# Projections and experts' gate/up in products of 512 columns instead of 256

## The reference

```
def swiglu(h, w_gate, w_up, w_down):
    return (jax.nn.silu(h @ w_gate) * (h @ w_up)) @ w_down
```

## Time and profile before

| | |
|---|---|
| median of 3 runs | 2544.52 us (2544.34 to 2544.85) |
| the profiled execution's own time | 2551.51 us |
| its span, first to last instruction | 2549.70 us, mean granted TensorE clock 0.966 |
| TensorE matmul busy | 2403.7 us (94%) |
| VectorE busy | 1775.0 us (70%) |
| ScalarE busy | 1316.0 us (52%) |
| GpSimd busy | 190.2 us (7%) |
| read from memory | 539.03 MB, 212 GB/s over the span |

### The profile page before, as it was taken

One profiled execution on the slowest core, in us unless ns is written; L12 is line 12 of the kernel. 1 busy time (PEld: TensorE's weight loads), 2 busy tenths in 40 slices (PEclk: granted clock), 3 DMA queues, 4 the chain that ended last, 5 costly groups with the idle time before them and its releaser, 6 DMA issues. The chain is left out here.

```text
span 2549.7 us, 45461 instructions
## 1 busy us (share of the span) xinstructions
PE 2403.7 (94%) x17555; PEld 2189.1 (86%) x17555; DVE 1775.0 (70%) x2869; ACT 1316.0 (52%) x2067; POOL 190.2 (7%) x168
## 2 busy tenths in 40 slices
PE   7889999999998999999899998888999999999998
PEld 6877789889988789989789988578999999999997
DVE  4655665556566465565755567548999999999997
ACT  2245244343443544442444442337877877777775
POOL 1310000000004000008100013000000000000000
PEclk9898999999999999999899997799999999999999
DMA  8510655646544054534045451027999999999995
GB/s 356 231 67 34 250 188 220 232 168 223 218 154 149 1 188 174 195 132 161 6 149 196 176 212 51 1 92 287 357 337 345 356 346 334 353 345 332 355 343 204
DMA packets 82234, 542.93 MB, mean 213 GB/s; under 512 B 9329, under 2 KB 9841, under 8 KB 33905
## 3 DMA queue, kind: packets, MB, share of 16 engines
q1 hardware_dynamic: 79184, 529.57, 56.2%
q10 hardware_dynamic: 2848, 10.55, 1.1%
HBM read 539.03 MB, written 1.05 MB: 212 GB/s over the span
## 5 line engine op out<-in xcount | busy, mean ns | idle before, releaser
L880 PE MATMUL bank<-w_hi,src_hi 128*128 128x256 f32 x2320 | 667.1, 288 | 26.5 <-DVE src_lo L646 14.4
L881 PE MATMUL bank<-w_lo,src_hi 128*128 128x256 f32 x2320 | 660.2, 285 | 0.0
L882 PE MATMUL bank<-w_hi,src_lo 128*128 128x256 f32 x2320 | 659.7, 284 | 0.0
L3373 DVE TENSOR_TENSOR w_lo<-ring,w_hi 128x1024 fp32r<-128x1024 f32 x528 | 637.0, 1220 | 31.9 <-ACT w_hi L3301 21.1
L880 PEld LDWEIGHTS bank<-w_hi,src_hi 128*128 128x128 f32 x2320 | 444.8, 192 | 46.3 <-issue 31.9
L881 PEld LDWEIGHTS bank<-w_lo,src_hi 128*128 128x128 f32 x2320 | 445.7, 192 | 7.2
L882 PEld LDWEIGHTS bank<-w_hi,src_lo 128*128 128x128 f32 x2320 | 445.8, 192 | 0.7
L880 PE MATMUL bank<-src_hi,w_hi 128*128 128x256 f32 x1472 | 423.8, 288 | 10.7 <-DVE src_lo L646 10.1
L1162 ACT ACTIVATE w_hi<-ring 128x1024 fp32r<-128x1024 f32 x260 | 274.2, 1057 | 295.3 <-PE bank L882 274.5
L1236 DVE TENSOR_TENSOR w_lo<-ring,w_hi 128x1024 fp32r<-128x1024 f32 x260 | 317.9, 1223 | 148.2 <-ACT w_hi L1162 147.7
L881 PE MATMUL bank<-src_lo,w_hi 128*128 128x256 f32 x1472 | 417.9, 284 | 0.0
(11 more groups left out here) (439 smaller groups left out, 2874.4 us busy)
## 6 DMA issues: line engine op xcount, KB each, us to landing
ring<-in_moe SPq DMA_DIRECT2D x176, 1024.0 KB, 7.3
ring<-in_ffn SPq DMA_DIRECT2D x66, 1536.0 KB, 6.7
ring<-in_moe SPq DMA_DIRECT2D x176, 512.0 KB, 6.9
ring<-in_ffn_ev SPq DMA_DIRECT2D x22, 1536.0 KB, 6.7
oT<-in_w_ada SPq DMA_DIRECT2D x20, 1024.0 KB, 6.1
big<-in_w_ada SPq DMA_DIRECT2D x20, 1024.0 KB, 8.7
ring<-in_w_in SPq DMA_DIRECT2D x18, 1024.0 KB, 8.5
ring<-in_w_out SPq DMA_DIRECT2D x12, 1024.0 KB, 8.0
```

The lines of the kernel that those rows point to most:

```text
L880: pe.matmul(out, ah, bh, start=start and i == 0, stop=False, skip_group_check=True)
L881: pe.matmul(out, ah, bl, start=False, stop=False, skip_group_check=True)
L882: mm = pe.matmul(out, al, bh, start=False, stop=stop and i == n - 1, skip_group_check=True)
L3373: dve.tensor_tensor(wl, piece, wh.bitcast(F32), ALU.subtract).then_inc(p.w_lo[kind].sem, 1)
```

## The change

Half as many matmuls, twice as wide, in two places.

In `linear`, the token chunks are taken in pairs (`wide = n_tok // 2`; a last odd chunk stays at 256 columns). A pair shares two banks of 512 columns; the first ring slot of a pair holds contraction tiles 0 to 3 of 512 columns, the second tiles 4 to 7, and a half `q` is two tiles of 512 columns instead of four of 256. `chunk_ready` and `chunk_taken` count pairs. The first pair is made tile by tile over four halves, of which the third and fourth are split after the source. TensorE waits for the gate's spreading after half 4 rather than after chunk 0, and the riders of chunk 0 stand behind half 4, those of chunk 2 behind half 6. VectorE takes out 512 columns at a time. In the layer-1 keys and values, the norm's `inline` work starts at chunk 1 rather than 0.

In `moe`, features are taken in pairs of steps: the even step makes contraction tiles 0 to 3 and the odd step tiles 4 to 7 of 256 gate and 256 up columns. Tanh, the three small VectorE operations, the activation's high part and its turn are done once for a pair. The down products of a pair stand behind each other in the odd step. The wait for the output of the job before stands in step 3 rather than 2. On the host the weights are laid out to match; bytes and packet sizes are the same.

```diff
@@ linear
+    wide = n_tok // 2
+    nu = n - wide
...
+            for q in range(4):
+                pe.wait_ge(*p.w_lo[q % 3](q // 3 + 1))
+                for i in (2 * q, 2 * q + 1):
+                    pe.wait_ge(*src_ready(front.ready[i]))
+                    for m in range(2):
+                        mm = product(q, i, m)
+                mm.then_inc(p.w_used[q % 3].sem, 1)
+            pe.wait_ge(*p.w_used[0](2))
             pe.sem_inc(ready.sem, 1)
             if gate is not None:
                 spread_pe(p, pe, diag)
-                pe.wait_ge(*p.sig("gate_spread")(2))
-            for r in at.get(0, ()):
-                rider_product(p, pe, r)
+            for q in range(4, 2 * n):
+                c, b, i0 = q // 2, q % 3, first_of(q)
+                per = 2 if c < 2 * wide else 4
...
-                if h:
+                if q % 2 and ends(c):
                     pe.wait_ge(*p.w_used[b](q // 3 + 1))
                     pe.sem_inc(ready.sem, 1)
...
+                if q == 4 and gate is not None:
+                    pe.wait_ge(*p.sig("gate_spread")(2))
+                if q < 8:
+                    beside_slot(q - 4)
+                elif q % 2:
+                    beside_slot(c)
@@ ctx_heads1
-    first = 1 if queries else 0
+    first = 1
@@ moe, TensorE
-                    mm = products(pe, p.ps[2 + k % 2][:, 0:2 * P],
-                                  [((srcH[:, 4 * half + q, hs], srcL[:, 4 * half + q, hs]),
-                                    (wh[:, q, :], wl[:, q, :])) for q in range(4)], half == 0, half == 1)
+                    mm = products(pe, p.ps[2 + k // 2 % 2][:, :],
+                                  [((srcH[:, k0 + q, hs], srcL[:, k0 + q, hs]), (wh[:, q, :], wl[:, q, :]))
+                                   for q in range(2)], k0 == 0, k0 == 6)
...
-                if there(r, 1, first):
-                    turn_act(i, k - 1, first and r == 1)
-                if r == 2 and not first:
+                if r % 2 == 0 and there(r, 2, first):
+                    turn_act(i, k // 2 - 1, first and r == 2)
+                if r == 3 and not first:
                     pe.wait_ge(*job_at(y_kept, i, 2, 2 * b))
-                if there(r, 2, first):
+                if r % 2 and there(r, 3, first):
+                    down(i, k - 3)
                     down(i, k - 2)
@@ moe, ScalarE
+                if r % 2 and there(r, 3, first):
+                    hi_down(k - 3)
+                    act.wait_ge(*pair_at(a_turned, i, c + 1))
+                    act.wait_ge(*at(p.w_used[DOWN], i, 2 * c))
+                    act.activation(p.actH[:, :], p.ps[4][:, 0:T], ACT.Copy).then_inc(act_hi.sem, 1)
+                    hi_down(k - 2)
@@ moe, VectorE
+                if r % 2 and there(r, 3, first):
+                    lo(k - 3, down_piece(k - 3), DOWN)
+                    dve.wait_ge(*pair_at(act_hi, i, c + 1))
+                    dve.tensor_tensor(p.actL[:, :], p.ps[4][:, 0:T], p.actH[:, :].bitcast(F32),
                                       ALU.subtract).then_inc(act_ready.sem, 1)
+                    lo(k - 2, down_piece(k - 2), DOWN)
```

More of the change, by code:

```diff
@@ L975, in _ @@
                     start_loads(p, act, loads)
-                if q == 4 and gate is not None:
+                if q == 6 and gate is not None:
                     spread_act(p, act, p.gates[:, 0, :])
@@ L994, in product, with first_of, beside_slot @@
                     pair = (wh[:, ms], wl[:, ms]), (p.srcH[:, k, :], p.srcL[:, k, :])
[L995 to L1006, removed]
+                return products(pe, p.ps[2 * (unit(c) % pairs_of_banks) + m][:, 0:cols], [pair], i == 0, i == KT - 1)
+            def first_of(q):
+                c = q // 2
+                return 2 * (q % 4) if c < 2 * wide else 4 * (q % 2)
+            def beside_slot(c):
+                if side is not None and c == n - 3:
+                    pe.wait_ge(*sided(1))
+                    side_product(p, pe, p.ps[6])
+                if side is not None and c == n - 2:
+                    side_turn(p, pe, p.ps[7])
+                for r in at.get(c - 1, ()):
+                    rider_turn(p, pe, r)
+                for r in at.get(c, ()):
+                    rider_product(p, pe, r)
+            for q in range(4):
[6 more added lines that the diff above has]
+            pe.wait_ge(*p.w_used[0](2))
             pe.sem_inc(ready.sem, 1)
@@ L1060, in _ @@
                         low(q)
[L1061 to L1077, removed]
@@ L1078, in _ @@
-                ins.then_inc(taken.sem, 1)
+                if ends(c):
+                    u = unit(c)
+                    c0, cols = (c - 1, 2 * PC) if c < 2 * wide else (c, PC)
+                    dve.wait_ge(*ready(u + 1))
+                    if u == 0 and gate is not None:
+                        dve.wait_ge(*p.sig("gate_spread")(2))
+                    for m in range(2):
+                        bank = p.ps[2 * (u % pairs_of_banks) + m][:, 0:cols]
+                        cut = slice(c0 * PC, c0 * PC + cols)
+                        if c >= n_tok:
+                            ins = dve.tensor_copy(out_feat[:, 2 * (c - n_tok) + m, :], bank)
+                        elif residual is None:
+                            w = min(cols, out.shape[2] - out_at[c0])
+                            ins = dve.tensor_copy(out[:, m, out_at[c0]:out_at[c0] + w], bank[:, 0:w])
+                        elif gate is None:
+                            ins = dve.tensor_tensor(residual[:, m, cut], residual[:, m, cut], bank, ALU.add)
+                        else:
+                            y = p.work[:, m * cols:m * cols + cols]
+                            chain(dve.tensor_tensor(y, bank, p.gates[:, 0, cut], ALU.mult))
+                            ins = dve.tensor_tensor(residual[:, m, cut], residual[:, m, cut], y, ALU.add)
+                    ins.then_inc(taken.sem, 1)
@@ L1089, in _ @@
                 if inline is not None:
+                    if ends(c):
+                        dve.wait_ge(*taken(unit(c) + 1))
                     inline(dve, chain, c)
@@ L1097, in _ @@
                 dve.tensor_copy(side, p.ps[7][:, 0:NT * NE].rearrange("p (m n) -> p m n", m=NT))
-    ready.passed(n)
-    taken.passed(n)
+    ready.passed(nu)
+    taken.passed(nu)
     if side is not None:
@@ L2249, in inline @@
     def inline(dve, chain, c):
-        if c in (2, 3):
-            square_sums(p, chain, dve, keys[c - 2], p.work[:, 0:256], st[:, 4 * (c - 2):4 * (c - 2) + 4])
         if c == 3:
+            for w in range(2):
+                square_sums(p, chain, dve, keys[w], p.work[:, 0:256], st[:, 4 * w:4 * w + 4])
             mean_squares(p, dve, st, HD)
@@ L3319, in step @@
                     keep_job(i, b + 1, GATHER_AT.index(r - 3))
-                m = k - 2
-                if there(r, 2, first):
-                    act.wait_ge(*loaded_at(p.dn_loaded, 0, i, m))
-                    act.wait_ge(*at(p.w_used[DOWN], i, m - 1))
-                    act.activation(sets[m % 2][0][:, DOWN, :], down_piece(m), ACT.Copy).then_inc(p.w_hi[DOWN].sem, 1)
                 if r == FC + 2:
@@ L3385, in step @@
-                if r < FC:
-                    lo(k, side_piece(k, 1), 1)
-                if there(r, 2, first):
-                    dve.wait_ge(*at(half_ready, i, m + 1))
-                    if not (first and r < 4):
-                        dve.wait_ge(*at(a_turned, i, m - 1))
-                    dve.scalar_tensor_tensor(out=aJ[:, m % 2, :], in0=zz[:, m % 2, :], scalar=0.5, in1=bank[:, P:2 * P],
-                                             op0=ALU.mult, op1=ALU.mult).then_inc(a_ready.sem, 1)
@@ L3405, in step @@
                     keep_rest(i, b + 1, GATHER_AT.index(r - 4))
-                m = k - 2
-                if there(r, 2, first):
-                    lo(m, down_piece(m), DOWN)
                 if r == FC + 2:
```

132 lines of the change are left out of this document (68 added, 64 removed).

## The result

The changed kernel takes 2531.35 us (median of 8 runs, 2523.87 to 2538.73) against 2544.43 for the kernel before beside it (8 runs, 2542.87 to 2549.66): a ratio of 0.9943, interval 0.9933 to 0.9953. By the ratio that is 14.5 us less, by the two medians 13.1. 27 were forecast, so about half of the forecast gain came. The time lies inside the range, and beside what rival A gives (2531).

What follows compares the result with a forecast made beforehand. TensorE was taken as the bound, with VectorE and DMA close behind in the experts. Projections -13.0 and experts -14 us sum to -27, giving 2517.5 us; range 2499 to 2537.

Steps and rivals of the forecast that it cites:

- rival A: Experts gain nothing because VectorE's low parts come too slowly and the DMA share is 0.93: 2531 us, 17%.
- Bound and price in the projections: Projections: TensorE alone is the bound, 512 columns cost 0.2285 us; columns give -14.9 us, the projections in all -13.0.
- Riders: Projections: riders closer together wait for a megabyte's load and VectorE's adding; +3 us, bounds -2 to +10.
- If TensorE waits at the riders for their load: Projections: a sign that would show the prediction wrong in the changed profile; no size of its own.
- Job start: Experts: TensorE stands 2.0 us for the activation's low part, with restart 2.3, where 1.2 stood; bounds 1 to 5.
- Pair of steps: Experts: gate and up, two turns and 12 downs take 8.44 us a pair, with no stall inside.
- Ends of the range in the experts: Experts: -14 us, ends -26 (0.227 us a matmul, no more stop) and +8 (0.2325, 5 us stops).
- C: Experts: the pair's own chain, turn to high part to low part, makes VectorE stand; slower, 2571 us, 10%.
- D: All widened matmuls: 512 columns cost nearly two of 256, 0.2375 us; no change, about 2545 us, 4%.
- E: Riders and tails eat the projections' gain, the experts keep theirs: 2530 us, 7%.

Runs made afterwards that it cites:

- e1: Changed kernel with the experts and their weight layout put back to the kernel before, so only the projections change: 2536.7 us, ratio 0.996.
- e3: Changed kernel with ScalarE's take-out of the old output put ahead of the down weights and activation in a job's step 3: 2512.7 us, ratio 0.9866.
- e6: e3 with the experts' loads cut to an eighth of their bytes, computing with stale weights: own time 2509.3 us, jobs of 97.98 us.
- e9: e6 with ScalarE's and VectorE's weight splits also cut to 256 of 1024 columns after the first job: own time 2511.5 us.
- e2: Changed kernel with the projections put back to the kernel before, so only the experts' gate and up change: 2545.8 us, ratio 0.999.

## Why the prediction was right or wrong

- **Bound and price in the projections: right.** 0.2270 us a matmul in a long run, 0.54 and 0.30 at a pair's end, no idle by `gates` before half 5 (three times 0.69 us before). Measured alone, 10 us (6 to 14) against 13.
- **Riders: mis-sized.** The term was +3 us. x's projection took 52.2 us where it had taken 49.7 (first product to next front), although its columns and stops had become 2.4 us cheaper, so the cost there alone was about 5: a wait of 2.50 us and, in this profile, 6.8 us of half clock behind it. With 3.4 us of half clock, in e1, the same projection took 50.5. The context's took 55.0 where it had taken 56.4. The place of the waits and a load as their source were foreseen, but not the half clock, nor that the load is a chunk of the projection's own weights, held in SP's queue behind the riders' loads, nor that it reaches TensorE by way of VectorE's low parts. "If TensorE waits at the riders for their load" stood among the signs of being wrong, and it came close to happening.
- **Job start: right.** 2.0 us was forecast, with restart 2.3; the first start came 2.32 us after the start before it, for the reason given, and with the take-out first it went without a successor. What was missed is the half clock behind it, two times in six jobs, 1.6 us each, 0.5 us a job.
- **Pair of steps: mis-sized, and this is what failed.** "A pair of steps is 24 x 0.2285 = 5.48, two turns 0.22, 12 downs 2.74: 8.44." In e3, with no wait, turns lie 8.55 us apart. 24 x 0.2317 = 5.56, 12 x 0.2306 = 2.77 and 0.22 are those 8.55, so the whole error is the price of a 512, (0.0032 x 264 + 0.0021 x 132) = 1.1 us a job. The 0.22 came out right by luck: the two turns take only 0.14 of their own, and the filling behind them, which the prediction had counted before the change and dropped after it, is the rest: the first 512 behind a turn is followed after 0.316 us instead of 0.232, so 0.084. With the half clock that is 1.7 of the 1.8 us a job that were missing.
- **Ends of the range in the experts.** 0.2325 stood as the dear end; only the dense SwiGLU's rows were looked at, and the experts' own `down` of 512 columns, in the trace of before, was not. It already ran at 0.231 there, as in these two starts with four distances between them (0.93 us):
```profile
2049.11 0.39 PE L881 MATMUL bank<-w_lo,act_hi 128*128 128x512 f32 x1
...
2050.04 0.39 PE L882 MATMUL bank<-w_hi,act_lo 128*128 128x512 f32 x1
```
- **Rivals.** A's number, 2531, is the result, but its reasons (VectorE's low parts, the DMA share) are refuted by e6 and e9, so that the number agrees is luck. C did not happen: no wait inside a pair. D was wrong for the projections, and in the experts it was a third right: a 512 cost 0.2317 us, where 0.2285 was forecast and D had 0.2375. E was wrong in its split: the projections kept their gain but for the riders, and the experts lost theirs.

## What to carry to other kernels

The price of a wider matmul has to be read where the kernel will run it: the same 512 columns were 0.2265 us apart with one set of operands and 0.232 with another, and that was half of the saving (from 0.238 for two of 256 columns). When an engine is busy throughout and still slower than its own rows elsewhere, list its distances by place in the repeating pattern before suspecting its neighbours; a pattern that stays the same within some nanoseconds whatever the load belongs to its own order and addresses. When products are moved to a later place, look also at which loads wait for them and what stands behind those loads in the queue. And when steps are doubled, look at what is taken out once a period: it must be queued ahead of the instruction that waits for the new, longer step, or the wait is paid in full, and the clock may charge for it again.

## What the runs showed of the hardware

- The place of the weights' parts in SBUF changes the distance of fp32r matmuls of 512 columns: 0.2317 us with parts that began 576, 576, 0 and 64 bytes behind a multiple of 2048, 0.2279 with all at 576. Which operand or which distance matters is open: both parts of the set were moved at once. The Trainium skill (TensorE: Matmul & The Clock Gate, "Step-by-step: what each phase is for") says that streaming and weight loading have read ports of their own and don't take bandwidth from each other; no run here shows what happens between them, but something of the operands' place does reach the pace.
- After a restart the first distance is 0.305 to 0.316 us and about 5 to 10 more lie between 0.224 and 0.236 before they settle at 0.2265.
- Idle times of TensorE of 1.93 to 2.16 us at the seven job starts (2.3 to 2.55 us between two starts) were followed by 3.4 us of half clock in two of seven cases in the changed kernel and in three of seven in e2, and by none in the others. Such a stretch cost 1.4 to 1.6 us of the job.
- The changed kernel's runs lie 15 us apart, those of the kernel before 7; the projections' change alone has it (2526.7 to 2542.5), and the take-out edit did not lessen it. The scatter goes with TensorE's mean granted clock in each run: in e3 0.970 in the two runs of 2504 and 2505 us and 0.964 in those of 2518 and 2520; in e1 0.971 in the fastest and 0.963 in the slowest. As an estimate, 0.006 of 2510 us is 30 us more at half clock, and at 1.6 us for every 3.4 us that makes 14 of the 16 us. Where in the kernel those stretches lie, and why the change in the projections brings more of them in some runs, no run here shows.
